# A causal mask applied on TensorE: one rounded-format product per bank ahead of the scores in place of two float32 products behind them

## The reference

```python
ss = jnp.einsum('bqghd,bgqkd->bghqk', qs, kg).astype(jnp.float32) * SCALE
ps = jax.nn.softmax(jnp.where(mask_s[:, :, None], ss, NEG_INF), axis=-1)
o_slc = jnp.einsum('bghqk,bgqkd->bqghd', ps.astype(vg.dtype), vg)
...
mask_w = (diff >= 0) & (diff < WINDOW) & (kpos[None, :] >= 0)
sw = jnp.einsum('bqghd,bkgd->bghqk', qs, kwb).astype(jnp.float32) * SCALE
pw = jax.nn.softmax(jnp.where(mask_w, sw, NEG_INF), axis=-1)
```

## Time and profile before

| | us |
|---|---|
| median of three runs | 2783.22 |
| lowest and highest | 2780.2, 2786.68 |
| profiled execution, its own time | 2782.16 |
| its span in the trace | 2779.9 |
| PE busy | 2642.2 (95%) |
| DVE busy | 1092.0 (39%) |
| ACT busy | 879.1 (32%) |

### The profile page before, as it was taken

The page is one execution under the profiler, slowest core; times in us unless marked ns, Lnnn a source line. Parts: engine busy times, 40 slices in busy tenths (PEclk is TensorE's granted clock), DMA queues, the critical chain, the costliest instruction groups (busy, mean ns, idle before and its releaser), DMA issues.

```text
span 2779.9 us, 31962 instructions
## 1 busy us (share of the span) xinstructions
PE 2642.2 (95%) x13096; PEld 1762.9 (63%) x13096; DVE 1092.0 (39%) x1717; ACT 879.1 (32%) x1379; POOL 55.8 (2%) x110
## 2 busy tenths in 40 slices
PE   7998979999998889999999999699999999999997
PEld 6877658878876578887888877544343343443433
DVE  4545355554554455466666544511111111111112
ACT  4435324444444244432234454211111111111111
POOL 0000000000000000000010000000000000000000
PEclk9999889999999899999999999789999999999999
DMA  6544445544455445343331234569999999999999
GB/s 245 185 180 170 164 184 183 187 174 182 182 179 198 174 174 194 140 152 125 121 122 61 91 131 151 202 279 425 429 428 429 428 428 429 429 428 429 428 428 416
DMA packets 51739, 700.88 MB, mean 252 GB/s; under 512 B 5874, under 2 KB 6258, under 8 KB 9248
## 3 DMA queue, kind: packets, MB, share of 16 engines
q1 hardware_dynamic: 48640, 688.26, 61.5%
q0 software_dynamic: 3008, 11.33, 1.2%
HBM read 696.43 MB, written 1.05 MB: 251 GB/s over the span
## 4 chain that ended last, share of the span: by engine, by line
PE 91%; DVE 5%; ACT 2%; DMA 1%; issue 1%; POOL 0%; SPq 0%; DVEq 0%; ACTq 0%; POOLq 0%
PE bank L396 39%; PE bank L2602 24%; PE bank L1710 6%; PE bank L2549 4%; PE bank L2616 2%; PE bank L2592 2%; DVE split_r L373 1%; ACT split_r L364 1%; PE bank L2043 1%; DMA ring<-in_stream 1%; PE bank L2021 1%; PE bank L649 1%; PE bank L919 1%; PE bank L1095 1%; PE bank L1873 1%
## 5 line engine op out<-in xcount | busy, mean ns | idle before, releaser
L396 PE MATMUL bank<-split_r,xT_r 128*128 128x512 f32 (+1 forms) x2880 | 672.9, 395 | 32.7 <-DVE xT_r L567 10.1
L373 DVE TENSOR_TENSOR split_r<-ring,split_r 128x2048 fp32r<-128x2048 f32 (+1 forms) x200 | 455.0, 2276 | 522.2 <-ACT split_r L364 522.0
L396 PEld LDWEIGHTS bank<-split_r,xT_r 128*128 128x128 f32 x2880 | 545.3, 193 | 148.8 <-issue 26.0
L364 ACT CAST split_r<-ring 128x2048 fp32r<-128x2048 f32 (+1 forms) x200 | 378.8, 1896 | 536.1 <-PE bank L396 533.6
L396 PE MATMUL bank<-split_r,work_r 128*128 128x512 f32 x1920 | 462.2, 400 | 0.0
L396 PEld LDWEIGHTS bank<-split_r,work_r 128*128 128x128 f32 x1920 | 360.4, 188 | 93.8 <-issue 7.2
L2602 PE MATMUL bank<-ring,work 128*64 128x512 f32 x1536 | 344.3, 597 | 1.4 <-DVE work L2566 1.4
L2602 PEld LDWEIGHTS bank<-ring,work 128*64 128x64 f32 x1536 | 107.9, 138 | 229.6 <-issue 229.6
L2602 PE MATMUL bank<-split,work 128*64 128x512 f32 x1024 | 232.2, 595 | 0.0
L1710 PE MATMUL bank<-work,ring 128*128 128x256 f32 x896 | 200.9, 379 | 0.0
L2652 DVE TENSOR_SCALAR work<-bank 128x512 f32<-128x512 f32 x32 | 22.1, 692 | 427.8 <-PE bank L2616 427.8
(11 more groups left out here) (336 smaller groups left out, 2026.5 us busy)
## 6 DMA issues: line engine op xcount, KB each, us to landing
ring<-in_stream SPq DMA_DIRECT2D x224, 2048.0 KB, 9.1
split<-in_stream SPq DMA_DIRECT2D x66, 2048.0 KB, 15.3
work<-in_stream SPq DMA_DIRECT2D x33, 2048.0 KB, 13.8
ring<-in_stream SPq DMA_DIRECT2D x6, 1024.0 KB, 5.5
row<-in_rows POOLq DMA_DIRECT2D x6, 512.0 KB, 4.0
ring<-in_stream SPq DMA_DIRECT2D x2, 1120.0 KB, 7.1
work<-in_conv POOLq DMA_DIRECT2D x2, 768.0 KB, 5.8
x<-in_x SPq DMA_DIRECT2D x1, 1024.0 KB, 5.2
```

What stands on the lines that cost most here:

```text
L364: act.copy(hi, self.part(half)).then_inc(*up("half_hi", half.h))
L373: dve.tensor_tensor(lo, self.part(half), hi.bitcast(F32), ALU.subtract).then_inc(*(self.freed_up(half.chunk.c) if half.ends_chunk else up( ...
L396: mm = self.nc.tensor.matmul(out, a[x][a_at], w[y][w_at], start=start and n == 0, stop=stop and n == 2)
```

## The change

- In the first FFN of layer 0, ScalarE copies the identity and the causal triangle into the last part of the work area in the rounded format (two 128x128 copies), behind its rope work, and signals that. An assertion keeps the mixer's tiles clear of that place.
- `pe_scores` of units 0 and 1 waits for that signal.
- For each bank one fp32r product of the identity with the triangle, read twice over (256 columns), writes the masked block of both heads of the bank, as the first of its accumulation. In m = 1 units it stands behind the 4 scores of the first key block.
- The scores of a block are issued for all four heads in turn; those of the masked block add to what the mask product wrote.

```diff
+        self.causal_r = self.work_r[:, WORK - 432:WORK - 176]
...
             if i == 1 and not self.before:
                 self.act_rope()
                 self.act_silu_c()
+                act.wait_ge(*at("rope", 1))
+                act.copy(self.causal_r[:, 0:P], self.ident)
+                act.copy(self.causal_r[:, P:2 * P], self.const("causal")[:, P:2 * P]).then_inc(*up("causal", 0))
...
-        assert at[0] <= WORK, at[0]
+        assert at[0] <= WORK - 432, at[0]
...
-        diag = self.const("causal")[:, P:2 * P]
         if i >= 2:
             pe.wait_ge(*at("p", st, i - 2))
-        for pair in range(2):
-            for kb in range(m + 1):
-                c0 = pair * SEQ + kb * P
-                for hh in (2 * pair, 2 * pair + 1):
-                    h = 4 * g + hh
-                    r = self.head_rows(h)
-                    pe.matmul(bank[2 * (i % 2) + hh % 2][:, c0:c0 + P], self.qT[1][r, h // 2, m * P:(m + 1) * P],
-                              self.kT[r, 2 * b + g, kb * P:(kb + 1) * P], start=True, stop=kb < m)
-            for hh in range(2):
-                mm = pe.matmul(bank[2 * (i % 2) + hh][:, c0:c0 + P], self.ident, diag, start=False, stop=True)
+        else:
+            pe.wait_ge(*at("causal", 0))
+        for kb in range(m + 1):
+            if kb == m:
+                for hh in range(2):
+                    own = bank[2 * (i % 2) + hh][:, :].rearrange("p (a k n) -> p a k n", a=2, k=MT)[:, :, m, :]
+                    pe.matmul(own, self.causal_r[:, 0:P], spread(self.causal_r[:, P:2 * P], 1, 2), start=True, stop=False)
+            for hh in range(4):
+                h, c0 = 4 * g + hh, hh // 2 * SEQ + kb * P
+                r = self.head_rows(h)
+                mm = pe.matmul(bank[2 * (i % 2) + hh % 2][:, c0:c0 + P], self.qT[1][r, h // 2, m * P:(m + 1) * P],
+                               self.kT[r, 2 * b + g, kb * P:(kb + 1) * P], start=kb < m, stop=kb < m or hh >= 2)
         mm.then_inc(*up("scores", st, i))
```

## The result

| | us |
|---|---|
| before, median of 6 runs | 2783.4 (2779.73 to 2786.68) |
| changed, median of 6 runs | 2759.74 (2759.42 to 2764.68) |
| ratio | 0.9926, 95% interval 0.9915 to 0.9936 |
| changed, profiled execution: time, span | 2759.74, 2757.5 |

The change saves 0.74%, by the interval 18 to 24 us; the forecast was 10.8 us and the range ended at 2765. The direction was right, the size was not: the profiled executions lie 22.4 us apart.

The account below looks back on a forecast made before the run. TensorE was taken as the bound, with 91% of the chain of waits. Savings of 4.1, 1.2 and 9.7 us made 15.0, less 4.2 for bg products: 10.8 us saved, forecast 2772.4 us, range 2765 to 2780.

Parts of the forecast that it names:

- Where the chain runs: Mixers: units 0, 1, 4, 5 and 7 lie on the chain in both layers; units 2, 3 and 6 give nothing.
- the second rival: Units 5 and 7 hidden behind ScalarE, VectorE or a weight chunk: only 3.8 us saved, 2779.4; chance 0.15.
- The setup: Two 128x128 copies on ScalarE in the first FFN: no cost, since ScalarE next sits idle 2.03 us.
- Price of the mask products: In each unit's masks: a 256-column product costs 0.13 us at full clock, 0.22 us at the lower clock.
- the term of 1.02 us per m = 1 unit: Units 0 and 1, full clock: 1.28 - 2 x 0.13 = 1.02 us saved each, 4.1 us over both layers.
- The third rival: Mask products in the new format cost as float32 records, 0.32 us per 128 columns: 0.6 us saved, 2782.6; chance 0.06.
- The charge on bg part 0: Longer PE idle ahead of both bg products drops their clock: 2.1 us lost each, 4.2 us together.
- Net: 15.0 - 4.2: Whole kernel: 15.0 us saved on the chain less 4.2 us charged to the bg products, 10.8 us faster.
- The rule I set against the change: Gaps between matmul bursts halve the clock; applied to PE's longer idle ahead of the bg products, charged 4.2 us.
- The slower rival: Without dense mask work the clock falls from unit 0 to the bg product's end: 13.6 us slower, 2796.8; chance 0.05.
- Range: Kernel time from 2765 (no clock charge, cheapest product) to 2780 us (late units hidden), leaving out the last two rivals.

Follow-up runs that it names:

- e2: Changed kernel with the new form only in units 0, 1, 4, 5 and 7, old form elsewhere: 2760.19 us, ratio 0.9922 to the kernel before.
- e1: Changed kernel with the new form only in units 2, 3 and 6, old form elsewhere: 2783.47 us, ratio 1.0004 to the kernel before.
- e4: Changed kernel with each wide mask product issued twice: 2765.93 us, ratio 0.9945 to the kernel before.
- e8: Changed kernel with 8 more wide mask products in each of units 0 and 1: 2767.57 us, ratio 0.9952 to the kernel before.
- e3: Changed kernel with the new form only in unit 4, old form elsewhere: 2777.82 us, ratio 0.9987 to the kernel before.
- e10: Changed kernel with 18 filler products in PE's wait ahead of bg part 0: 2759.64 us, ratio 0.9921 to the kernel before.
- e9: Changed kernel with 36 filler products in PE's wait ahead of xc part 0: 2761.86 us, ratio 0.993 to the kernel before.
- e11: Changed kernel with fillers in the waits ahead of xc part 0, compression and bg part 0: 2757.76 us, ratio 0.991 to the kernel before.

## Why the prediction was wrong, point by point

- *Where the chain runs*: right. e2 has the whole gain, e1 none; nothing on VectorE, ScalarE or the queues came up to hide units 5 and 7 (the second rival). The setup cost nothing: the casts took 0.30 and 0.29 us, and ScalarE still had 1.64 us idle.
- *Price of the mask products*: the term of 1.02 us per m = 1 unit was 0.86 (1.72 for two). A single product was priced well (0.12 measured, 0.13 taken, and at the lower clock 0.215 from e4's 2.29 against 1.86, 0.22 taken), but the pair's one change between full and half rows, 0.2 us, was left out. At the lower clock units 5 and 7 gave 1.90 against 1.94: there the run of 8 scores took 1.18 us where I had 1.38, which made up for it. Unit 4 gave 1.63, since its last four mask records cost 0.88 us from start to start ahead of the full-row bg products where I had 1.15. So 13.5 us direct for 15.0. The third rival is out.
- *The charge on bg part 0*: the idle grew to 2.74 and 2.87 us (forecast 3.0 and 3.9), and both bg products slowed, by 1.5 us each (forecast 2.1). Right as far as it went.
- **The step that failed**: "Net: 15.0 - 4.2" took the clock everywhere else as given. I had seen that 5 units run at the lower clock, and let only their price depend on it, not whether they would still be there. The clock elsewhere gave 11.0 us (8.0 net of the bg charge; the 0.75 us wait in layer 1 comes on top). In parts: the compression kept the clock across the same 2.94 us gap because the work ahead of it was 1.7 us shorter (8.71 us again with that work put back, e8), where xc part 0 had taken 7.8 us or more; and between bg part 0 and bg part 1 the light work is 1.6 us shorter (unit 4, at equal clock), and the clock comes back sooner (e3: 0.6 to 0.9 us of bg part 1 a layer; e2, e10). That in the changed kernel the fall misses that stretch altogether goes with the fall in the idle before it, but no run shows why: in e8 too the stretch ran at full clock behind such a fall, in e1 and e9 it did not.
- *The rule I set against the change* (the Trainium skill, "TensorE: Matmul & The Clock Gate", section Why this matters for your kernels: no idle gaps between bursts). It fits the gap before the compression as it was (0.50 after 2.94 us), but the changed kernel kept 1.00 across the same 2.94 us, and as a price it misled: filling one gap (e10) gave 0.1 us (ratio 0.9921 against 0.9926), and filling another (e9) ended 2 us higher in the median, because the fall moved to the next light place. Only all three together (e11) gave something. The slower rival, built on the same idea, went the other way: less dense work, and a higher clock (71.0 us at the lower level for 86.8).
- *Range*: it took in the loss of the charge but no gain of the clock. With one stretch at the lower clock in each mixer either lost or kept, +-4 us a layer was possible: compression 1.5, bg part 1 1.6, unit 4 0.8. The kernel before showed bg part 1 (7.2 against 5.6 us for bg part 0) and unit 4 (3.49 against 2.13 for layer 1's unit 5) at either level; the compression's full-clock time is known from the later runs only.

## What to carry to other kernels

Where a trace shows stretches of the lower clock on the chain, removed work in or ahead of them can move the clock's fall and rise as well as its own time; put both signs of that into the range, from the rows of the same block at either level where the trace has both. A price for a product is a price per run of like products: count the changes between kinds too, here 0.2 us each, which with its share of the clock made the order alone worth 11 us (7 to 15). And test an idle gap by filling it before charging for it.

## What the runs showed that I had not expected

- The changes between half-row and full-row products: 0.19 us, in the fits of 4 and 8 records (0.42 and 0.65 us; 0.64 and 1.09 us) and of 2 and 4 wide products (0.43 and 0.67 us). What in the array takes that time no run tells apart.
- The fall behind an idle of 2.94 us is not given by its length: the same gap before the same compression left the clock at 1.00 or took it to 0.50. PE in windows in the changed kernel, where the earlier trace rows had 0.50:

```profile
282.00:283.00 1.00, 1.00 (x12) 1.00 0.92 184
283.00:284.00 1.00, 1.00 (x14) 1.00 0.86 268
```

- What exactly decides whether a gap or a light stretch costs the clock stays open. The runs show that it hangs on how long the work before it lasted (e8) and on how xc part 0 ran. A fall in bg part 0 came with a light stretch at full clock in the changed kernel and e8 (4 mixers of 4), and with one in which the clock fell again in e1 and e9 (4 of 4). They don't give the rule.
